# Dense SwiGLU layer of a two-layer decoder: three rounded products per weight tile replaced by plain fp32 products on four column tiles

## What is computed

```python
def dense_swiglu(h, w_in, w_out):            # h 256x1024, w_in 1024x5632, w_out 2816x1024
    g, u = jnp.split(h @ w_in, 2, axis=-1)
    return (jax.nn.silu(g) * u) @ w_out
...
h = layer_norm(ALPHA * h + mix, ln_g[l, 0], ln_b[l, 0])
if l % 2 == 0:
    ffn = dense_swiglu(h, dense_w_in[l // 2], dense_w_out[l // 2])
h = layer_norm(ALPHA * h + ffn, ln_g[l, 1], ln_b[l, 1])
```

## Time and profile before

| | us |
|---|---|
| median of 3 runs (lowest, highest) | 1339.75 (1337.9, 1342.03) |
| the profiled execution, its own time | 1337.99 |
| its span, first to last instruction | 1336.2 |
| PE busy with matmuls / weight loads | 1309.3 / 721.6 |
| DVE busy / ACT busy | 396.5 / 281.2 |
| dense layer, first product to the transposes behind it | 171.2 to 355.5 |
| turns of experts | 453.1 to 1322.9 |

### The profile page before, as it was taken

How to read it: one execution, slowest core, us unless ns; L and a number is a source line. 1 busy time by engine, 2 the same in 40 slices (tenths; PEclk the granted TensorE clock), 3 DMA queues, 4 the chain that set the end, 5 groups by cost and what they waited for, 6 DMA issues and landing times.

```text
span 1336.2 us, 31629 instructions
## 1 busy us (share of the span) xinstructions
PE 1309.3 (98%) x14086; PEld 721.6 (54%) x14086; DVE 396.5 (30%) x681; ACT 281.2 (21%) x510; POOL 75.8 (6%) x104
## 2 busy tenths in 40 slices
PE   9998999999999999999999999999999999999996
PEld 6765788888776534533633543443453363354344
DVE  6569666664676411010101101101101010120222
ACT  5456465553455200000010010000000001000001
POOL 2033200000022200000000000000000000000100
PEclk9999999999999999999999999999999999999999
DMA  9680358955542999999999999999999999999992
GB/s 324 196 220 33 126 192 326 332 189 191 158 140 96 379 397 421 417 399 420 418 398 420 419 402 398 419 418 394 420 417 372 420 418 392 408 419 417 418 420 103
DMA packets 115774, 443.16 MB, mean 332 GB/s; under 512 B 11936, under 2 KB 49088, under 8 KB 101312
## 3 DMA queue, kind: packets, MB, share of 16 engines
q1 hardware_dynamic: 108704, 423.39, 81.7%
q10 hardware_dynamic: 5792, 13.63, 2.8%
q0 software_dynamic: 1152, 4.19, 0.8%
HBM read 425.85 MB, written 15.34 MB: 330 GB/s over the span
## 4 chain that ended last, share of the span: by engine, by line
PE 93%; DVE 3%; ACT 2%; SPq 1%; issue 1%; DMA 0%; DVEq 0%; ACTq 0%
PE bank L1731 43%; PE bank L1724 22%; PE bank L1586 6%; PE bank L1142 4%; PE bank L1144 4%; PE bank L1143 4%; PE bank L1589 3%; PE bank L1159 1%; PE bank L1463 1%; PE bank L1424 1%; ACT arena L948 1%; PE bank L1332 1%; PE bank L1172 1%; DMA ring<-in_w_in_a_dram 0%; ACT wh L770 0%
## 5 line engine op out<-in xcount | busy, mean ns | idle before, releaser
L1731 PE MATMUL bank<-ring,arena 128*32 128x448 f32 x2880 | 275.0, 539 | 0.0
L2226 DVE TENSOR_TENSOR arena<-arena,bank 128x448 f32<-128x448 f32 x48 | 26.9, 617 | 727.8 <-PE bank L1731 727.8
L1731 PEld LDWEIGHTS bank<-ring,arena 128*32 128x32 f32 x2880 | 93.4, 110 | 173.9 <-issue 172.6
L1772 DVE TENSOR_TENSOR wl<-ring,wh 128x2048 fp32r<-128x2048 f32 (+1 forms) x54 | 121.7, 2259 | 55.4 <-ACT wh L770 55.1
L1724 PE MATMUL bank<-ring,arena 128*32 128x256 f32 x2304 | 125.8, 379 | 0.0
L1586 PE MATMUL bank<-hT,wh 128*128 128x512 f32 x344 | 121.6, 399 | 0.0
L770 ACT ACTIVATE wh<-ring 128x2048 fp32r<-128x2048 f32 (+1 forms) x56 | 105.5, 1888 | 37.7 <-PE bank L1144 30.7
L1731 PE MATMUL bank<-wls,arena 128*32 128x448 f32 x1152 | 111.2, 539 | 0.0
L1731 PE MATMUL bank<-whs,arena 128*32 128x448 f32 x1152 | 111.2, 539 | 0.0
L1088 ACT ACTIVATE arena<-bank 128x448 f32<-128x448 f32 x48 | 22.6, 544 | 388.8 <-PE bank L1731 388.8
L1724 PEld LDWEIGHTS bank<-ring,arena 128*32 128x32 f32 x2304 | 74.9, 110 | 52.0 <-issue 3.9
(11 more groups left out here) (293 smaller groups left out, 1294.6 us busy)
## 6 DMA issues: line engine op xcount, KB each, us to landing
ring<-in_moe_w_in_dram SPq DMA_DIRECT2D x120, 896.0 KB
ring<-in_moe_w_out_dram SPq DMA_DIRECT2D x48, 1024.0 KB
whs<-in_moe_w_in_dram SPq DMA_DIRECT2D x48, 896.0 KB, 17.9
wls<-in_moe_w_in_dram SPq DMA_DIRECT2D x48, 896.0 KB, 18.1
arena<-in_moe_w_in_dram SPq DMA_DIRECT2D x32, 896.0 KB, 16.0
whs<-in_moe_w_out_dram SPq DMA_DIRECT2D x24, 1024.0 KB, 21.3
wls<-in_moe_w_out_dram SPq DMA_DIRECT2D x24, 1024.0 KB, 22.3
ring<-in_dense_w_in_dram SPq DMA_DIRECT2D x22, 1024.0 KB
```

Source lines behind the costliest of these rows:

```text
L1731: ins = pe.matmul(bank[s + GROUPS * (kind == "u")][32 * j:32 * j + 32, 0:BLOCK], xgT[:, c, 32 * s:32 * s + 32], slot[:, BLOCK * j:BLOCK * ...
L1772: dve.tensor_tensor(wl[:, n % SPLITS, 0:size], slot_of(n)[:, 0:size], wh[:, n % SPLITS, 0:size].bitcast(F32), ALU.subtract).then_inc(split, 1)
L2226: ins = dve.tensor_tensor(act[:, s, :], act[:, s, :], bank[GROUPS + s][:, 0:BLOCK], ALU.mult)
```

## The change

What it does:

- `whole` names the items `dense_in` and `dense_out` too: ACT and DVE no longer split these 33 items, and SP may load their slots again only when PE has used them.
- h is turned into `hTf` in plain fp32: three of the four banks by ACT (`turn_plain`), one by DVE; `lower_h`, `move_low` and the rounding go at this place. The seven matmuls without use that stood behind `lower_h` stand ahead with the first one, 8 in a row.
- `dense_in`: each step (j, k) is four matmuls of 256 columns, one for each 32-column tile of the array, stationary operand 32 weight columns from the ring, moving operand `hTf[:, k, :]`, the same for all four. Both blocks j lie in one bank, and gate and up of piece c go to banks 2(c % 2) and 2(c % 2) + 1. PE waits only for the pieces of c - 2.
- `dense_out`: each (tt, half, j) is four matmuls of 512 columns on the column tiles, stationary 32 tokens of `act_dense`, moving operand the same 512 weight columns for all four.
- Behind each pair of items ACT takes silu straight from the bank and DVE multiplies it with the other bank into `act_dense`; the copies, sums and halves go.
- Nothing outside the dense layer and the turns of h ahead of it is changed.

```diff
 def whole(n):
-    return n < N_FIRST and ITEMS[n][0] == "cmp"
+    return n < N_FIRST and ITEMS[n][0] in ("cmp", "dense_in", "dense_out")
...
-        for first, banks, movers in ((T_X, (4, 5, 6, 7), "vvvv"), (T_H1, (4, 5, 6, 7), "aavv"),
+        for first, banks, movers in ((T_X, (4, 5, 6, 7), "vvvv"), (T_H1, (4, 5, 6, 7), "aaav"),
...
+            def turn_plain(q, tt):
+
+                act_e.wait_ge(turned, T_H1 + 2 * tt + q + 1)
+                act_e.activation(hTf[:, 4 * q:4 * q + 4, tt * P:tt * P + P],
+                                 bank[TBANK[T_H1 + 2 * tt + q]][:, :].rearrange("p (c n) -> p c n", c=4), ACT.Copy)\
+                     .then_inc(moved_a, 1)
...
-            for c in range(N_DENSE + 1):
...
+            for c in range(N_DENSE):
+                act_e.wait_ge(used, AT["dense_in"] + 2 * c + 1)
+                if c >= 2:
+                    act_e.wait_ge(act_ready, c - 1)
+                act_e.activation(silu[:, c % 2, :], bank[2 * (c % 2)][:, :], ACT.Silu).then_inc(silu_ready, 1)
...
             next_h(0, T_H1, 0)
-            keep_warm(7, 1)
-            lower_h(0, T_H1)
-            keep_warm(7, 7)
+            keep_warm(7, 8)
             next_h(0, T_H1, 1)
             keep_warm(3, 2)
...
             for c in range(N_DENSE):
                 for gu in range(2):
-                    if c >= 1:
-                        pe.wait_ge((gate_summed, up_summed)[gu], c)
                     n = AT["dense_in"] + 2 * c + gu
+                    if c >= 2:
+                        pe.wait_ge((silu_ready, act_ready)[gu], c - 1)
                     ready(n)
-                    wts = both(n, DC)
+                    wts = slot_of(n).rearrange("p (c n) -> p c n", c=DC)
                     for j in range(2):
...
                         for k in range(DC):
-                            pe.matmul(bank[2 * gu + j], wts[0][:, k, P * j:P * j + P],
-                                      hT[:, k, :, :].rearrange("p a n -> p (a n)"), start=(k == 0), stop=False,
-                                      skip_group_check=True)
-                            ins = pe.matmul(rest, wts[1][:, k, P * j:P * j + P], hTh[:, k, :], start=False,
-                                            stop=(k == DC - 1), skip_group_check=True)
+                            if n == AT["dense_in"] and j == 0 and k % 4 == 0:
+                                moved(pe, T_H1 + k // 4)
+                                moved(pe, T_H1 + 2 + k // 4)
+                            for s in range(4):
+                                ins = pe.matmul(bank[2 * (c % 2) + gu][32 * s:32 * s + 32, SEQ * j:SEQ * j + SEQ],
+                                                wts[:, k, P * j + 32 * s:P * j + 32 * s + 32], hTf[:, k, :],
+                                                start=(j == 0 and k == 0), stop=(j == 1 and k == DC - 1), skip_group_check=True)
                     ins.then_inc(used, 1)
...
-                    pe.wait_ge(act_low, c + 1)
-                wts = both(n, 2)
+                    pe.wait_ge(act_ready, c + 1)
+                wts = slot_of(n).rearrange("p (c n) -> p c n", c=2)
                 for half in range(2):
                     for j in range(2):
-                        ins = product(bank[4 + 2 * half + tt][:, :],
-                                      [t[:, 2 * c + j, tt * P:tt * P + P] for t in (actTh, actTl)],
-                                      [t[:, j, 512 * half:512 * half + 512] for t in wts],
-                                      False, (c == N_DENSE - 1 and j == 1))
+                        for s in range(4):
+                            ins = pe.matmul(bank[4 + 2 * half + tt][32 * s:32 * s + 32, :],
+                                            act_dense[:, 2 * c + j, tt * P + 32 * s:tt * P + 32 * s + 32],
+                                            wts[:, j, 512 * half:512 * half + 512], start=False,
+                                            stop=(c == N_DENSE - 1 and j == 1), skip_group_check=True)
...
+            for c in range(N_DENSE):
+                dve.wait_ge(silu_ready, c + 1)
+                dve.wait_ge(used, AT["dense_in"] + 2 * c + 2)
+                dve.tensor_tensor(act_dense[:, 2 * c:2 * c + 2, :], silu[:, c % 2, :].rearrange("p (a n) -> p a n", a=2),
+                                  bank[2 * (c % 2) + 1][:, :].rearrange("p (a n) -> p a n", a=2), ALU.mult).then_inc(act_ready, 1)
```

More of the change, by code:

```diff
@@ L284, in decoder_kernel @@
             .rearrange("p (k n) -> p k n", n=512)
-        actTh = room(0, FF // P, SEQ, of=arena_r)
-        actTl = room(5632, FF // P, SEQ, of=arena_r)
+        act_dense = room(0, FF // P, SEQ)
         silu = room(11264, 2, 512)
@@ L359, in decoder_kernel @@
         h_ready = sem("h_ready")
[L360 to L363, removed]
         silu_ready = sem("silu_ready")
         act_ready = sem("act_ready")
-        act_high = sem("act_high")
-        act_low = sem("act_low")
         router_wide = sem("router_wide")
@@ L971, in preload, with move_low @@
                      .then_inc(preloaded, 1)
-            def move_low(first, k):
+            def move_low(first):
                 for q in range(2):
-                    act_e.wait_ge(lowered, 2 * k + q + 1)
+                    act_e.wait_ge(lowered, q + 1)
                     act_e.activation(hTl[:, 4 * q:4 * q + 4, 0:P],
@@ L1004, in norm_part @@
                         act_e.activation(pre[:, 0, cols], pre[:, 0, cols], ACT.Copy, scale=std[:, 0, 1:2]).then_inc(pre_scaled, 1)
-                if k < 2:
+                if k == 0:
+                    for q in range(2):
+                        turn_plain(q, 0)
+                elif k == 1:
                     turn_h(first, 0)
@@ L1017, in norm_part @@
                     load_norm(k + 1)
[L1018 to L1021, removed]
+                elif k == 0:
+                    turn_plain(0, 1)
+                    act_e.wait_ge(h_ready, 4)
+                    load_norm(k + 1)
+                elif k == 1:
+                    move_low(first)
+                    split_weights(AT["q_b"] + 2)
                     turn_h(first, 1)
@@ new lines, in _ @@
+            for c in range(N_DENSE):
[3 more added lines that the diff above has]
+                act_e.activation(silu[:, c % 2, :], bank[2 * (c % 2)][:, :], ACT.Silu).then_inc(silu_ready, 1)
+                if c == 2:
+                    moved(act_e, T_H1 + 3)
+                    for half in range(2):
+                        for tt in range(NT):
+                            preload(4 + 2 * half + tt, tt, half)
+                if c == 3:
+                    act_e.wait_ge(zeros_ready, 1)
+                    for half in range(2):
+                        act_e.dma_start(xb.rearrange("(s p) n -> p s n", p=P)[:, :, 512 * half:512 * half + 512],
+                                        zeros.rearrange("p (s n) -> p s n", s=1).to_broadcast([P, GROUPS * NE * CAP // P, 512]))\
+                             .then_inc(zero_filled, 16)
@@ L1515, in next_h, with lower_h @@
                     ins.then_inc(turned, 1)
-            def lower_h(k, first):
+            def lower_h(first):
                 pe.wait_ge(nident_ready, 1)
                 for q in range(2):
-                    pe.wait_ge(high, 4 * (k + 1) + q + 1)
+                    pe.wait_ge(high, 4 + q + 1)
                     pe.matmul(bank[TBANK[first + q]][:, :].rearrange("p (c n) -> p c n", c=4), nident[:, :],
@@ L1612, in _ @@
             keep_warm(3, 1)
-            lower_h(1, T_H2)
+            lower_h(T_H2)
             out_banks_free(0, len(PROJ_A))
@@ L2111, in norm @@
                     scale(k, tt)
-                if k < 2:
+                if k == 0:
+                    dve.wait_ge(turned, first + 4)
+                    dve.tensor_copy(hTf[:, 4:8, P:2 * P], bank[TBANK[first + 3]][:, :].rearrange("p (c n) -> p c n", c=4))\
+                       .then_inc(moved_v, 1)
+                elif k == 1:
                     turn_h(first)
```

38 lines of the change are left out of this document (removed).

## The result

The changed kernel takes 1383.43 us in the median of 3 runs (1382.93 to 1384.49) where the kernel before takes 1339.75: slower by 43.7 us, a ratio of 1.0326 with a 95% interval of 1.0299 to 1.0354. The forecast was 1383.0 us.

What follows compares the result with a forecast made beforehand. PE, busy throughout the dense layer, was taken as the bound: dense_in 152.0 us plus dense_out 75.5 us replace 184.3 us, +43.2, all other terms nothing, giving a median of 1383.0 us, range 1376.5 to 1391.

Steps and rivals of the forecast that it cites:

- The bound: Dense layer: PE is busy 100% and never waits, so work taken off ACT and DVE gains nothing.
- The price of a group: Four plain fp32 tile matmuls in the dense layer: 431.7 ns for 256 columns, 858.4 ns for 512, from the experts' rows.
- Way in: Ahead of the dense layer: DVE's relief and dropping lower_h bring h no sooner; nothing, if anything 0.2 us.
- Way out: Behind dense_out: the first 128 tokens' norm runs beside the second's products, the second norm starts as before; nothing.
- banks: Waits between items: silu 0.62 us and product 0.69 us are covered; nothing, even without alternate banks.
- weights: Dense weight transfers: SP runs six items, 41 us, ahead, longer than the zeros' 26.2 us; nothing.
- The loads: Dense groups: one column tile's loads run beside another's matmuls, as in the experts, costing nothing more.
- loads in line: Rival, dense products: a tile's new stationary columns stop the array; 114 us more, 1497 us; chance 0.02.
- The upper bound: Dense groups priced as the compression product (L1332), 450 ns a step: change +51.1 us, 1389.1 us.
- the rival with the shared operand: Dense groups: tiles sharing one moving operand hinder each other, 530 ns a pair; +43 us, 1426 us; chance 0.05.
- the faster rival: Dense products: one shared stream halves the pace of column tiles; layer 113.8 us, -70.5 us, 1269 us; chance 0.02.
- my expectation of e1: Full-array products in the dense layer: 58 to 104 ns more each, +26 to +46 us over the changed kernel, 1409 to 1430 us.

Runs made afterwards that it cites:

- e7: Kernel before, with the 256-column matmul of the weights' rounded rest left out in the dense layer's first half, all splits still made: 1307.74 us, ratio 0.9766.
- e4: Changed kernel with gate always in bank 0 and up always in bank 1 in the dense layer's first half, no alternation: 1382.7 us.
- e1: Changed kernel with each group of four column tiles made one plain fp32 matmul over the full array, in both dense halves: 1383.59 us, ratio 1.0325 to before.
- e2: Changed kernel with groups of two tiles of 64 columns in place of four of 32: 1382.0 us, ratio 1.0317 to before.
- e8: Changed kernel, each dense_in group made two full-array products of 128 moving columns, stationary columns loaded again: 1387.34 us.
- e5: Changed kernel, each four-tile group of 256 columns in dense_in made two four-tile groups of 128, stationary columns loaded again: 1412.85 us.

## Why the prediction was right, point by point

- **The bound.** PE alone before, PE alone after. e7 shows how much room ACT and DVE had.
- **The price of a group.** 431.7 ns forecast from the earlier trace rows, 152.08 / 352 = 432.0 measured. For 512 columns, extrapolated from two widths, 858.4 forecast, 75.53 / 88 = 858.3 measured. The sum for the layer was 227.5, measured 227.6. That agreement is the forecast's merit. That the median came within 0.4 us is in part luck: the three runs of before lie 4.1 us apart, and from the profiled execution I had said 1381.2, which came as 1384.49.
- **Way in.** Forecast as nothing, and it is nothing: from the first transposes on every step comes 1.73 us later than before, the shift of the start, the first dense product too. PE waits longer for h (1.30 us in the row of its loads, for 0.25 in the earlier trace rows), with `lower_h` gone, and begins no sooner:

```profile
171.20 0.42 PEld L1502 LDWEIGHTS bank<-ident,h 128*128 128x128 f32 x4 [1.30 <-DVE h L2061]
171.87 0.42 PEld L1502 LDWEIGHTS bank<-ident,h 128*128 128x128 f32 x4 [0.24 <-DVE h L2061]
```

- **Way out, banks, weights.** No wait at any of them; e4 tests the banks alone. The zeros took 30.7 us to land in place of 26.2, still under the 41 us that the ring covers.
- **The loads.** The experts' rows were right: nothing beyond 432.0 ns a group. The Trainium skill, "TensorE: Matmul & The Clock Gate", "Part 3: Packing small matmuls — row/col tiling", has loads beside matmuls only where the row group differs. Here eight loads of 110 ns pass in 432 ns though all tiles use all rows, and in e1 loads of the whole array are hidden too. The trace speaks against that rule in both forms. The same part of that page of the Trainium skill also names a background weight buffer, and a load into it goes ahead of matmuls in flight; the runs agree with that. The 645 ns that the prediction gives as the sign of loads in line is worked out from the load time on that page of the Trainium skill; by the earlier trace rows it would have been 692. 432 ns excludes both.
- **The upper bound was too wide, and for a wrong reason.** "As the compression product" took 450 ns from a stretch of eight steps, and the rival with the shared operand took 530 ns a pair from eight rows of L1424. e2 and e8 repeat the forms of L1332 and L1472 in long stretches, and by them such pieces hold 0.15 to 0.2 us that belong to the stretch and not to its rows. For L1424 no run did so. The argument against the faster rival used the same short pieces: the full array's 272 ns for 128 columns are 223 in e8. Its conclusion, that fewer streams are not quicker, holds. This did not touch the forecast, which rested on 96 and 84 groups; it did make my expectation of e1 wrong by 25 to 46 us, and that of e2 by 9.
- **The transposes behind** were forecast at about 398.5 us and came at 400.57; the 1.7 us of the start and the rounding of the sum are the difference.

## What to carry to other kernels

Price a product by columns times cycles, for all its passes. Three rounded passes cost 353 ns for 256 columns and 681 for 512; one plain fp32 product at four cycles a column costs 432 and 858. Cutting a full 128-wide product into column tiles gives nothing back, it only multiplies instructions. Take work off an engine only where PE waits for it; if PE is busy 100% of a stretch, that work is free until PE's own is cut. Take the price of a row from a stretch of several hundred rows at one pace. A piece of eight rows carries an edge of 0.15 us or more, which looks like a cost of the instruction, and even 128 rows of e5 show 28.9 ns a row where the long piece shows 27.85.

## What the runs showed of the hardware that I had not expected

- Plain fp32 over the full array and on four or two column tiles costs the same, 431.7 to 432.1 ns for 256 columns and 858 ns for 512 (e1, e2, the change).
- A full-array product of 128 plain fp32 columns with its stationary operand loaded each time runs at 111.7 ns a row (e8), 5 ns over its columns, though each load lasts 186 to 192 ns. The row of loads is busy without a break there (151.00 of 151.00 us), so shorter rows may show them; no run went further.
- At 5632 rows in 182 us (e5) PE stood still for 17.6 us in all, mostly after some 256 instructions or a multiple, for up to 3.05 us while another DMA filled the queues. The same sums in 1408 rows (e8), and those of the change in 2816, had no such gap. That the fetching of instructions is the cause was not tested by itself.
- The granted clock was low behind stands of PE: 0.53, near the level of 1.2 GHz, in the 4.8 us after 9.46 us without a matmul (e7), and 0.68 in the 5.4 us after each stop of 3.05 us (e5).
- The rounded matmuls of 512 columns pass at 227 ns, 14 ns over their columns, the plain ones over the full array at 2.5 ns a row over theirs with 256 and 512 columns (e1), and 5 ns with 128 (e8). Why the rounded ones pay more stays open; no run here varied it.
